# Gate tables of a gated delta rule made by head instead of by chunk

## The reference, cut to what matters

```python
g = jnp.cumsum(g, axis=-1)
decay = jnp.exp(jnp.where(tri, g[..., :, None] - g[..., None, :], -jnp.inf))
kk = jnp.einsum("bnhid,bnhjd->bnhij", k, k)
lmat = jnp.where(strict, beta[..., :, None] * kk * decay, 0.0)
...
qk = jnp.einsum("bnhid,bnhjd->bnhij", q, k) * decay
q_dec = q * jnp.exp(g)[..., None]
```

## Time and profile before

| What | Value |
|---|---|
| median of 3 runs | 1693.69 us (1691.41 to 1696.97) |
| the profiled execution's own time | 1695.34 us |
| its span | 1693.5 us |
| mean granted TensorE clock, as a share of 2.4 GHz | 0.989 |
| busy: PE, DVE, ACT, POOL | 1646.5, 822.4, 697.3, 902.4 us |

### The profile page before, as it was taken

The page is one execution under the profiler, slowest core; times in us unless marked ns, Lnnn a source line. Parts: engine busy times, 40 slices in busy tenths (PEclk is TensorE's granted clock), DMA queues, the critical chain, the costliest instruction groups (busy, mean ns, idle before and its releaser), DMA issues.

```text
span 1693.5 us, 23604 instructions
## 1 busy us (share of the span) xinstructions
PE 1646.5 (97%) x9487; PEld 1412.1 (83%) x9487; DVE 822.4 (49%) x1313; ACT 697.3 (41%) x1039; POOL 902.4 (53%) x515
## 2 busy tenths in 40 slices
PE   7999989999999999999999999999999999999997
PEld 7898988799889888888888878888887888888886
DVE  7778966733433101222111112127999953357744
ACT  6655544242322222234222223335534454366651
POOL 4455645243436445544555555448978656456661
PEclk9999999999999999999999999999999999999998
DMA  5476288553413234323333323333232423233332
GB/s 207 147 232 182 82 251 266 145 180 119 156 57 98 91 99 149 100 87 96 92 99 99 100 90 99 110 103 96 94 93 89 122 88 98 89 100 100 100 100 75
DMA packets 121268, 202.46 MB, mean 120 GB/s; under 512 B 32560, under 2 KB 71624, under 8 KB 121160
## 3 DMA queue, kind: packets, MB, share of 16 engines
q1 hardware_dynamic: 119400, 197.98, 37.6%
q10 hardware_dynamic: 1760, 2.98, 0.5%
HBM read 170.97 MB, written 29.97 MB: 119 GB/s over the span
## 4 chain that ended last, share of the span: by engine, by line
PE 86%; DVE 8%; ACT 3%; issue 2%; DMA 1%; SPq 1%; POOL 0%; DVEq 0%; ACTq 0%; POOLq 0%
PE ps L423 75%; PE ps L1813 4%; DVE cacc L2270 2%; DVE inv L637 1%; PE ps L945 1%; DVE prd L634 1%; PE ps L966 1%; PE ps L959 1%; PE ps L953 1%; PE ps L970 1%; DVE at L584 1%; PE ps L912 0%; DMA d_p<-dec 0%; PE ps L931 0%; PE ps L1517 0%
## 5 line engine op out<-in xcount | busy, mean ns | idle before, releaser
L411 POOL TENSOR_TENSOR w_lo<-w_raw,w_hi 128x1024 fp32r<-128x1024 f32 x264 | 633.4, 2408 | 453.8 <-ACT w_hi L405 453.6
L423 PE MATMUL ps<-hp,w_hi 128*128 128x512 f32 (+2 forms) x2432 | 596.5, 345 | 4.4 <-DVE cacc L2270 2.8
L423 PEld LDWEIGHTS ps<-hp,w_hi 128*128 128x128 f32 x2432 | 404.7, 190 | 58.6 <-issue 4.1
L423 PE MATMUL ps<-hp,w_lo 128*128 128x512 f32 (+2 forms) x1216 | 371.6, 343 | 0.0
L405 ACT ACTIVATE w_hi<-w_raw 128x1024 fp32r<-128x1024 f32 x264 | 277.3, 1053 | 155.1 <-DMA w_raw<-in_w 147.3
L423 PEld LDWEIGHTS ps<-hp,w_lo 128*128 128x128 f32 x1216 | 212.1, 190 | 25.9
L423 PE MATMUL ps<-n_hi,w_hi 128*128 128x512 f32 x464 | 184.1, 397 | 0.0
L423 PE MATMUL ps<-n_hi,w_lo 128*128 128x512 f32 x464 | 180.7, 389 | 0.0
L423 PE MATMUL ps<-n_lo,w_hi 128*128 128x512 f32 x464 | 180.5, 389 | 0.0
L1289 DVE SCALAR_TENSOR_TENSOR ps<-u_in,par,ps 128x511 f32<-128x511 f32 (+14 forms) x210 | 154.6, 739 | 6.5
L423 PEld LDWEIGHTS ps<-n_hi,w_hi 128*128 128x128 f32 x464 | 87.1, 188 | 19.7 <-issue 1.9
(11 more groups left out here) (417 smaller groups left out, 2625.7 us busy)
## 6 DMA issues: line engine op xcount, KB each, us to landing
w_raw<-in_w SPq DMA_DIRECT2D x264, 512.0 KB, 3.5
d_y<-zero SPq DMA_DIRECT2D x6, 688.0 KB, 6.0
d_x<-zero SPq DMA_DIRECT2D x6, 688.0 KB, 5.9
d_at<-at SPq DMA_DIRECT2D x16, 256.0 KB, 3.1
d_kc<-kc SPq DMA_DIRECT2D x16, 256.0 KB, 3.2
d_qd<-eg SPq DMA_DIRECT2D x16, 256.0 KB, 3.1
d_p<-dec SPq DMA_DIRECT2D x16, 256.0 KB, 3.3
AT<-d_at SPq DMA_DIRECT2D x16, 256.0 KB, 6.0
```

Source lines behind the costliest of these rows:

```text
L411: e.tensor_tensor(w_lo[:, u % RAW, :], w_raw[:, u % RAW, :], w_hi[:, u % RAW, :].bitcast(F32), ALU.subtract).then_inc(s_lo, 1)
L423: mm = e.matmul(ov, w, r[:, k, t0:t1], start=(first and n == 0 and p3 == 0), stop=(last and n == len(tiles) - 1 and p3 == 2))
```

## The change

The running sums are made once, as rows: right after `dk`, PE multiplies 32 columns of `gdec` (8 heads of one direction, and 24 that are not used) with the triangular matrices, eight fp32 products of 128 columns, into partitions 0 to 31 (forward) and 32 to 63 (backward) of bank 6, chunk by chunk along its 512 columns. ACT copies 64 rows of it to a rounded high part `gt_hi` (in the buffer of `on_rh0`, which is free until slot 9), DVE makes the remainder `gt_lo` ahead of tile 7's taps. `gdec` moves to a place of its own, longer by two blocks that are set to zero at the start.

A preparation x is now one head, x, with its four chunks. `pg` spreads that head's row over 128 partitions by two products of 512 columns (high and low part) per direction, in place of four fp32 products of 128. The counts and sizes of all other instructions stay. `pk` of head x waits for the q tile of that head, not for the half's last. The stores go out in the same sizes and order, to slots that now stand for a head; so the loads of the second stage pick one chunk out of four heads' slots: AT, X, Y still in pieces of 512 B, and KC, QD, PT in pieces of 512 B where it was 2 KB.

```diff
@@ -166,6 +166,8 @@
...
+        gt_hi, gt_lo = on_rh0, put("gt_lo", [P, SEQ], F32R)
+        gdec = put("gdec", [P, NB + 2, 2 * H])
@@ -188,7 +190,6 @@
...
-        gdec = z("gdec", [P, NB, 2 * H], tb + 320)
@@ -259,6 +260,14 @@
         def unit_rows(t, hf, slot):
...
+        def chunk_rows(t, hf, d, c):
...
+            return bass.AP(tensor=t, offset=((hf * 8 + 4 * d) * HG + c - 1) * USTEP, ap=[[P, P], [HG * USTEP, HG], [1, P]])
...
+        def chunk_cols(t, hf, d, c):
...
+            return bass.AP(tensor=t, offset=(hf * 8 + 4 * d) * P * HG * P + (c - 1) * P, ap=[[HG * P, P], [P * HG * P, HG], [1, P]])
...
         def unit_blocks(t, hf, slot, n):
@@ -332,7 +341,7 @@
...
-        pg = Signal(sem("s_pg"), ba=1, bat=1, dk=1)
+        pg = Signal(sem("s_pg"), ba=1, bat=1, dk=1, gt=1)
@@ -341,7 +350,7 @@
...
-        ga = Signal(sem("s_ga"), wba=1, sig=1, eA=1, ex=1, dk=3, lam=1, tap=TAPS - 1)
+        ga = Signal(sem("s_ga"), wba=1, sig=1, eA=1, ex=1, dk=3, gh=1, lam=1, tap=TAPS - 1)
@@ -357,7 +366,7 @@
...
-        dg = Signal(sem("s_dg"), halo=9, n2=1, zero=1, wlo=1, b=1, ch=20, lam=18, g2=2)
+        dg = Signal(sem("s_dg"), halo=9, n2=1, zero=1, wlo=1, b=1, ch=20, gl=1, lam=18, g2=2)
@@ -458,9 +467,12 @@
         def toks(c):
...
+        def chunks(t, h):
+            return t[:, h, META:T1].rearrange("p (c m) -> p c m", c=NCH)
...
         def pair_of(x):
...
-            return x // 4, HG * (x // 4), x % 4 + 1
+            return x // 4, x
...
         def spilled(e, sems, m):
@@ -500,50 +512,49 @@
...
-            e.scalar_tensor_tensor(gdec[:], t0, -1.0, ea, ALU.mult, ALU.mult).then_inc(dg.sem, 1)
+            e.scalar_tensor_tensor(gdec[:, 0:NB], t0, -1.0, ea, ALU.mult, ALU.mult).then_inc(dg.sem, 1)
...
         def pe_pg(e, x):
-            hf, h0, c = pair_of(x)
+            hf, h = pair_of(x)
...
-                    e.wait_ge(*ga.at("dk", 3))
+                    e.wait_ge(*dg.at("gl", 1))
...
-                for u in range(HG):
-                    g = gdec[:, c, d * H + h0 + u:d * H + h0 + u + 1].to_broadcast([P, P])
-                    mm = e.matmul(bankv(6 + d, P, P)[:, u], g, cmat("ub" if d else "uf"), start=True, stop=True)
-                mm.then_inc(m_gr.sem, 1)
+                pick = ident_r[0:64, BLK * d + h:BLK * d + h + 1].to_broadcast([64, P])
+                e.matmul(ps[:, 6 + d, :], pick, gt_hi[0:64, :], start=True, stop=False)
+                e.matmul(ps[:, 6 + d, :], pick, gt_lo[0:64, :], start=False, stop=True).then_inc(m_gr.sem, 1)
...
         def pe_pk(e, x):
-            hf, h0, c = pair_of(x)
-            e.wait_ge(*si.at("t", tile_of("q", h0 + HG - 1) + 1))
+            hf, h = pair_of(x)
+            e.wait_ge(*si.at("t", tile_of("q", h) + 1))
...
-            for u in range(HG):
-                mm = e.matmul(bankv(6, P, P)[:, u], kT[:, h0 + u, toks(c)], kT[:, h0 + u, toks(c)], start=True, stop=True)
+            for c in range(NCH):
+                mm = e.matmul(bankv(6, P, P)[:, c], kT[:, h, toks(c + 1)], kT[:, h, toks(c + 1)], start=True, stop=True)
...
-            for u in range(HG):
-                mm = e.matmul(bankv(7, P, P)[:, u], kT[:, h0 + u, toks(c)], qT[:, h0 + u, toks(c)], start=True, stop=True)
+            for c in range(NCH):
+                mm = e.matmul(bankv(7, P, P)[:, c], kT[:, h, toks(c + 1)], qT[:, h, toks(c + 1)], start=True, stop=True)
...
         def dve_pg(e, x):
-            hf, h0, c = pair_of(x)
+            hf, h = pair_of(x)
...
-                for u in range(HG):
-                    v = e.scalar_tensor_tensor(dec[:, d, u], bankv(6 + d, P, P)[:, u], gcol[:, c, d * H + h0 + u:d * H + h0 + u + 1],
+                for c in range(NCH):
+                    v = e.scalar_tensor_tensor(dec[:, d, c], bankv(6 + d, P, P)[:, c], gcol[:, c + 1, d * H + h:d * H + h + 1],
@@ -558,20 +569,20 @@
...
         def pool_pk(e, x):
-            hf, h0, c = pair_of(x)
+            hf, h = pair_of(x)
...
-            e.wait_ge(*si.at("t", tile_of("q", h0 + HG - 1) + 1))
+            e.wait_ge(*si.at("t", tile_of("q", h) + 1))
...
-                e.tensor_tensor(kc_b[hf][d][:], kT[:, h0:h0 + HG, toks(c)], eg[:, d], ALU.mult).then_inc(m_kc.sem, 1)
+                e.tensor_tensor(kc_b[hf][d][:], chunks(kT, h), eg[:, d], ALU.mult).then_inc(m_kc.sem, 1)
...
-                e.tensor_tensor(eg[:, d], qT[:, h0:h0 + HG, toks(c)], eg[:, d], ALU.mult).then_inc(m_qd.sem, 1)
+                e.tensor_tensor(eg[:, d], chunks(qT, h), eg[:, d], ALU.mult).then_inc(m_qd.sem, 1)
...
         def dve_pk(e, x):
-            hf, h0, c = pair_of(x)
+            hf, h = pair_of(x)
@@ -580,18 +591,18 @@
...
-                for u in range(HG):
-                    v = e.scalar_tensor_tensor(at_b[hf][d][:, u], bankv(6, P, P)[:, u], b2[:, c, d * H + h0 + u:d * H + h0 + u + 1],
-                                               dec[:, d, u], ALU.mult, ALU.mult)
+                for c in range(NCH):
+                    v = e.scalar_tensor_tensor(at_b[hf][d][:, c], bankv(6, P, P)[:, c], b2[:, c + 1, d * H + h:d * H + h + 1],
+                                               dec[:, d, c], ALU.mult, ALU.mult)
...
         def sp_pk(e, x):
-            hf, h0, c = pair_of(x)
+            hf, h = pair_of(x)
...
-                m, slot = 2 * x + d, 4 * d + c - 1
+                m, slot = 2 * x + d, 4 * d + h % HG
@@ -1053,7 +1064,6 @@
         def sp_level(e, s, k):
...
-            slot = 4 * s + c - 1
@@ -1066,18 +1076,17 @@
...
-            e.dma_start(SQ[s]["AT"][:], unit_rows(d_at, hf, slot)).then_inc(s_ld["AT"][s], 16)
+            e.dma_start(SQ[s]["AT"][:], chunk_rows(d_at, hf, s, c)).then_inc(s_ld["AT"][s], 16)
...
-            e.dma_start(SQ[s]["X"][:], unit_rows(d_x, hf, slot)).then_inc(s_ld["X"][s], 16)
+            e.dma_start(SQ[s]["X"][:], chunk_rows(d_x, hf, s, c)).then_inc(s_ld["X"][s], 16)
...
-            e.dma_start(SQ[s]["Y"][:], unit_rows(d_y, hf, slot)).then_inc(s_ld["Y"][s], 16)
+            e.dma_start(SQ[s]["Y"][:], chunk_rows(d_y, hf, s, c)).then_inc(s_ld["Y"][s], 16)
...
         def sp_chain(e, s, k):
...
-            slot = 4 * s + c - 1
@@ -1085,11 +1094,11 @@
...
-            e.dma_start(SQ[s]["KC"][:].rearrange("p u m -> p (u m)"), d_kc[hf, slot]).then_inc(s_ld["KC"][s], 16)
+            e.dma_start(SQ[s]["KC"][:], chunk_cols(d_kc, hf, s, c)).then_inc(s_ld["KC"][s], 16)
...
-            e.dma_start(SQ[s]["QD"][:].rearrange("p u m -> p (u m)"), d_qd[hf, slot]).then_inc(s_ld["QD"][s], 16)
-            e.dma_start(SQ[s]["PT"][:].rearrange("p u m -> p (u m)"), d_p[hf, slot]).then_inc(s_ld["PT"][s], 16)
+            e.dma_start(SQ[s]["QD"][:], chunk_cols(d_qd, hf, s, c)).then_inc(s_ld["QD"][s], 16)
+            e.dma_start(SQ[s]["PT"][:], chunk_cols(d_p, hf, s, c)).then_inc(s_ld["PT"][s], 16)
@@ -1575,6 +1584,12 @@
...
+                        g = gdec[:].rearrange("p c n -> p (c n)")
+                        for c in range(NCH):
+                            for d in range(2):
+                                o = 2 * H * (c + 1) + H * d
+                                mm = e.matmul(ps[BLK * d:BLK * d + BLK, 6, c * P:c * P + P], g[:, o:o + BLK], cmat("ub" if d else "uf"), start=True, stop=True)
+                        mm.then_inc(pg.sem, 1)
@@ -1906,6 +1921,8 @@
...
+                        e.wait_ge(*pg.at("gt", 1))
+                        e.activation(gt_hi[0:64, :], ps[0:64, 6, :], ACT.Copy).then_inc(ga.sem, 1)
@@ -2226,6 +2243,7 @@
...
+            e.memset(gdec[:, NB:], 0.0)
@@ -2263,6 +2281,9 @@
...
+                    if n == 7:
+                        e.wait_ge(*ga.at("gh", 1))
+                        e.tensor_tensor(gt_lo[0:64, :], ps[0:64, 6, :], gt_hi[0:64, :].bitcast(F32), ALU.subtract).then_inc(dg.sem, 1)
```

## The result

The changed kernel takes 1705.84 us (median of 11 runs, 1694.88 to 1713.25); the kernel before, in the same session, 1696.25 us (1691.41 to 1699.32, 11 runs). The ratio is 1.0047, 95% interval 1.0031 to 1.0063: slower, by 8 us by the ratio and 9.6 by the medians, where I had forecast 1693.9 us and no change. The spread is part of the result: 18 us where the kernel before has 8.

A forecast was written before the change was run, and what follows sets the result against it. PE looked full, but DVE and ACT paced 98 to 160 us, and a store wait with full DMA slots 0 to 2. Terms -1.0 + 0.8 + 0.4 = +0.2 on 1695.3 gave 1695.5, on the median 1693.9; range 1689 to 1698.6.

The forecast's parts named there:

- the clock paragraph: PE falls to 1.2 GHz after standing; shifted gaps may add or remove one slow stretch, 1.7 us either way.
- my sum: Tile stage -1.0, slot 0 +0.8, slot 2 +0.4 us: +0.2 us in all.
- Tile 6: Running sums as rows, ahead of tile 7: products taken as 0.9 us, tile 7's tap 0.9 us late.
- `pg`: Per preparation 0.92 us instead of 1.70; gains nothing in tiles 7 to 14, 0.20 us once in slots 0 to 2.
- `pk`'s own q tile: Tile 8: PE's 2.26 us gap goes; tile 9's taps on DVE start at 97.95, gaining 1.0 us.
- It survives to 160.8: The 1.0 us gained at tile 9 lasts to 160.8 us, since the chain until there is DVE's and ACT's.
- Loads in pieces: KC, QD, PT loads cost 0.18 us more per 256 KiB: 0.8 us in slot 0, 0.4 net in slot 2.
- PE-bound: Rival: PE bounds the first stage, so all its savings count: 9.2 us faster, 1684.5; chance 0.11.
- Gathered loads: Rival: loads before preparation 4's stores and in slots 0 to 3 are the bound: 1698.8 or 1701 us; chance 0.10.

The follow-up runs named there:

- e7: Kernel before, with the first part of DVE's substitution begun 3 us later, once: 1705.85 us, ratio 1.0056.
- e8: Kernel before, with the same one 3 us delay and POOL's splits of tiles 17 to 22 waiting for a DVE tap: 1698.41 us, ratio 1.0007.
- e3: Kernel before, with POOL's split of tiles 16 to 21 held until DVE has made its four taps of that tile: 1705.03 us, ratio 1.0047.
- e1: Changed kernel, with POOL's w_lo split of tiles 17 to 22 waiting until DVE has made one tap of that tile: 1696.45 us, ratio 0.9996.
- e9: Changed kernel, unaltered, timed again in another session: 1707.28 us, ratio 1.0052 to the kernel before.
- e6: Changed kernel, with each spread of a row made twice into the same bank: 1699.57 us, ratio 1.0021 to the kernel before.
- e2: Kernel before, with POOL's split of tiles 17 to 22 waiting for one DVE tap of that tile: 1695.64 us, ratio 0.9986.
- e12: e1's kernel, with preparation 0's wait for the last query head's tile put back: 1697.12 us, ratio 1.0001 to the kernel before.
- e11: e2's kernel, with DVE's n2 of the second half one tile later: 1692.38 us, ratio 0.9977 to the kernel before.
- e10: e1's kernel, with DVE's n2 of the second half one tile later: 1694.03 us, ratio 0.9991 to the kernel before.
- e5: Changed kernel, with preparation 0's PE and POOL parts again waiting for the last query head's tile: 1700.19 us, ratio 1.0016 to the kernel before.
- e4: e1's kernel, with KC, QD and PT stored in 512 byte pieces so their loads read 2 KB runs: 1701.50 us, ratio 1.0029 to the kernel before.

## Why the prediction was wrong

**The step that failed** is the clock paragraph: "A slow stretch may be entered once more or left once earlier: 1.7 us either way, which the range holds." I priced a slow stretch by PE's own time. By the rows it also set when POOL's split came, and so whether DVE's substitution was held up; the hold-ups were worth 7.4 to 9.5 us (e7 less e8, e3, e1 against after and e9). Behind it lies a second omission. I took tiles 17 to 23 as carried along unchanged, since the diff has no line in them, and did not read DVE's timeline past 162 us. The 2.38 us row at 205.56 stood there, and no rival had POOL in it. This omission is the part that the runs show (e1, e3, e7, e8); that the clock is what starts the series is argued from profiles. No term of my sum was above 1.0 us; I was adding small terms beside a stage with two paces, 6.3 to 7.3 and 8.0 to 8.8 us per tile.

The paragraph's first sentence was also too simple: after the same 2.84 us of standing, tile 17's product began at 1.2 GHz before and in e1, and ran at 2.4 GHz after and in e9.

*Tile 6*: 0.9 us taken; the sums take 1.0 us from start to start, and in e1 the first `at` is 0.97 us late (94.28, before 93.31). Right. After is 1.7 us late, but 0.7 of it was lost ahead of the sums, where both do the same work.

*`pg`*: 0.92 us taken, 1.1 measured, and no time gained by it directly. "Nothing" was right for what it saves, probably wrong as a whole: e6 suggests that the shorter spread changes how often the series occurs.

*`pk`'s own q tile*: PE's gap went, ACT's tap of tile 9 came at 95.70 us (forecast: before 96), DVE's taps without idle time; in e1 they start at 97.94 us (forecast 97.95). "It survives to 160.8" failed: the next `dec` waits for its store 1.20 us, in e1 1.11.

*Loads in pieces*: forecast 1.2 us in the slots. From slot 0 to slot 5 the kernel before takes 80.0 us and e2 81.6; e1 80.4, e9 81.8, e12 80.6; and e11 81.5, e10 82.3. The difference is lost among executions, at most a microsecond: right in size or somewhat high. The 5.7 us of the first profile are for the most part its own: its granted clock from 240 to 320 us was 0.89, before 0.98.

*The rivals.* PE-bound: no, 6.2 us less of PE work bought nothing. Gathered loads: 1701 us would have been the nearer number, for a wrong reason; e1 refutes it, with the same gathered loads at 1696.45 us. The forecast without hold-ups, +0.2 us, stands against +0.8 and +1.65 measured.

**Left open**: why e5 and e6 are still 3 to 4 us slower than the kernel before when few of their runs have the series (in e5's profile the loss lies behind the substitution, whose last copy is at 210.37 us, with a granted clock of 0.91 from 240 to 320 us); and what decides that the low clock falls at about 137 us (after, e9, e6, e10) or not (before, e1, e5; e12 and e4 have it there and in tile 17's product). e1's program is that of after up to tile 17's split, and yet the two profiles differ in it. The few runs of the kernel before above 1703 us (7 of 103 beside e1 to e12) may be the same series; none of them was profiled.

## What to carry to other kernels

A stage that the diff does not touch can still hold the price, if two engines in it exclude each other and only timing keeps them apart. Look for the one instruction that takes ten times its usual length beside another engine's, count how far the others are from it, and ask whether being late once makes an engine late again. Then let the schedule keep them apart with a wait, as e1 does, before judging any change by its time. And a profile shows one execution: where executions differ, as here by 18 us, one of each kind has to be read.

## What the runs showed of the hardware

DVE's instructions with two SBUF operands and POOL's 1024-column subtraction exclude each other: 0.22 to 0.43 us become 2.3 to 2.5. So does a DVE instruction with one SBUF operand and a constant, 0.17 us alone and 2.35 beside it. DVE's taps with PSUM as one operand aren't affected. A low clock on PE went with the faster kernel: where tile 17's product took 2.6 us longer, there was one hold-up and not six, and the hold-ups are worth 7.4 to 9.5 us. Stores in 512 byte pieces ran at 283 to 288 GB/s, where stores of the same data, three of four in 2 KB pieces, ran at 321 to 378. That one delay of 3 us locks the schedule into it for six tiles I had not expected.
